# Output projection of layer 0 moved into the latent attention, one tile late; 112 candidates and an even split of marks in the channel mixer

## The reference

```
out = jnp.concatenate([out_a, out_b], axis=-1) @ w_out
...
x = layer_norm(ALPHA * x + out, ln1_g[0], ln1_b[0])

# peer, per head: the 16 best of each half, then the 16 best of their sums
t1, i1 = lax.top_k(s1, PEER_TOPK)
t2, i2 = lax.top_k(s2, PEER_TOPK)
cand = t1[..., :, None] + t2[..., None, :]          # 16 x 16
top, sel = lax.top_k(cand, PEER_TOPK)
gate = jax.nn.softmax(top)
y = sum over k of gelu(x . u_tab[idx_k]) * gate_k * v_tab[idx_k]
```

## Time and profile before

| what | value |
|---|---|
| median of the runs | 4629.32 us (4619.73 to 4639.67) |
| the profiled execution | 4627.48 us, span 4625.8 us, mean granted clock 0.909 |
| busy share of the span | PE 83%, PEld 61%, DVE 62%, ACT 21%, POOL 34% |
| DMA | 1189.86 MB, mean 257 GB/s |
| attention, 581.8 to 1011.8 us | 430 us, PE busy 322.6 us |
| gap to the channel mixer, 1012 to 1145 us | 133 us, PE busy 77.4 us |

### The profile page before, as it was taken

One profiled execution on the slowest core, in us unless ns is written; L12 is line 12 of the kernel. 1 busy time (PEld: TensorE's weight loads), 2 busy tenths in 40 slices (PEclk: granted clock), 3 DMA queues, 4 the chain that ended last, 5 costly groups with the idle time before them and its releaser, 6 DMA issues. The chain is left out here.

```text
span 4625.8 us, 50127 instructions
## 1 busy us (share of the span) xinstructions
PE 3833.2 (83%) x17006; PEld 2823.3 (61%) x17006; DVE 2862.4 (62%) x6195; ACT 952.8 (21%) x2541; POOL 1559.2 (34%) x1334
## 2 busy tenths in 40 slices
PE   9788867767988799979889488768889799889885
PEld 4577733333866677757667344456667677667664
DVE  0256522312898988857777422345998987667767
ACT  0133111111121244301011112211212444101101
POOL 0012024310054365545555000000352655455552
PEclk9899979888999899989999799969999899999997
DMA  3100157762487899989999364404787999899995
GB/s 122 40 19 13 44 149 209 187 189 80 164 314 269 314 409 417 415 335 396 392 401 390 137 236 146 160 19 147 253 295 290 385 417 416 343 388 403 392 400 193
DMA packets 368972, 1189.86 MB, mean 257 GB/s; under 512 B 33988, under 2 KB 152389, under 8 KB 340749
## 3 DMA queue, kind: packets, MB, share of 16 engines
q0 software_dynamic: 159840, 570.77, 32.7%
q1 hardware_dynamic: 194174, 538.35, 32.2%
q10 hardware_dynamic: 14704, 77.55, 4.1%
HBM read 1094.29 MB, written 87.73 MB: 256 GB/s over the span
## 5 line engine op out<-in xcount | busy, mean ns | idle before, releaser
L1878 POOL DMA_INDIRECT peer_ru<-in_u_rows,peer_expert x512 | 793.0, 1549 | 1200.8 <-DVE peer_dot L2153 903.5
L1993 PE MATMUL peer_bank<-region,peer_v 128*128 128x288 f32 x4096 | 1032.0, 416 | 154.0 <-DMA peer_v<-in_v 117.9
L1946 PE MATMUL peer_bank<-peer_xT,peer_u 128*128 128x288 f32 x4096 | 1041.4, 412 | 43.5 <-ACT peer_hidden L2059 43.5
L1993 PEld LDWEIGHTS peer_bank<-region,peer_v 128*128 128x128 f32 x4096 | 798.9, 196 | 387.0 <-DMA peer_v<-in_v 124.3
L1946 PEld LDWEIGHTS peer_bank<-peer_xT,peer_u 128*128 128x128 f32 x4096 | 779.5, 193 | 253.2 <-issue 46.9
L2143 DVE SCALAR_TENSOR_TENSOR y<-peer_rv,peer_weight,y 128x1024 f32<-128x1024 f32 x512 | 655.0, 1279 | 139.6 <-ACT peer_weight L2009 101.9
L1886 POOL DMA_INDIRECT peer_rv<-in_v_rows,peer_expert x512 | 552.9, 1080 | 268.1 <-issue 137.5
L2153 DVE CUSTOM_DVE_ANT_0 peer_ru<-peer_ru,x 128x1024 f32<-128x1024 f32 x512 | 622.4, 1216 | 24.1 <-DMA peer_ru<-in_u_rows,peer_expert 23.5
L2007 ACT ACTIVATE peer_act_g<-peer_dot 128x1 f32<-128x1 f32 x512 | 103.4, 202 | 1217.8 <-DVE peer_dot L2153 1209.0
L2273 DVE TENSOR_TENSOR region<-region,peer_bank 128x288 f32<-128x288 f32 x496 | 219.6, 450 | 168.2 <-PE peer_bank L1993 166.0
L1868 POOL MEMSET y<- 128x1024 f32 x4 | 3.7, 951 | 728.5 <-POOLq L143 728.5
(11 more groups left out here) (491 smaller groups left out, 4385.2 us busy)
## 6 DMA issues: line engine op xcount, KB each, us to landing
peer_u<-in_uT SPq DMA_DIRECT2D x128, 1024.0 KB, 8.9
peer_v<-in_v SPq DMA_DIRECT2D x64, 2048.0 KB, 13.8
mlstm_w_in<-in_w_in_o SPq DMA_DIRECT2D x30, 1792.0 KB, 7.3
mla_keys<-in_keysT SPq DMA_DIRECT2D x256, 144.0 KB, 4.4
scratch_early<-peer_hidden ACTq DMA_DIRECT2D x64, 576.0 KB, 9.1
scratch_grids<-region ACTq DMA_DIRECT2D x24, 1536.0 KB, 10.4
region<-scratch_grids SPq DMA_DIRECT2D x32, 1152.0 KB, 28.2
region<-scratch_early SPq DMA_DIRECT2D x64, 576.0 KB, 7.5
```

The lines of the kernel that those rows point to most:

```text
L1878: pool.indirect_dma_start(ru[:, n % U_ROWS, :], None, u_rows, bass.IndirectOffsetOnAxis(ap=expert[:, T, k:k + 1], axis=0)).then_inc(ru_in[ ...
L1946: mm = mmul(bank[:, 4 + i % 2, 0:TD], u[:, h % URING, i % 2, k, :], xT[:, k, :], start=k == 0, stop=k == KD - 1)
L1993: mm = mmul(bank[:, SUM_BANKS[m % 6], 0:TD], v[:, g % 2, j, c * P:(c + 1) * P], w[:, g % 2, j, :], start=j == 0, stop=j == GI - 1)
```

## The change

In the attention: `mla` becomes `mla_layer`, which loads its constants itself and does the output projection of a tile inside the next one but one in its order (tile 0's inside tile 1, and so on; those of tile 3 and SAMP follow the loop). `x` is allocated from the start (the linear mixer's scratch tiles are laid into it), so that the store and load of `x_mid` go. `w_out` comes in parts of 256 columns (1 MB) through two buffers: 20 loads, the first 14 issued by ACT, the rest by SP. The key ring has 4 slots, `oT` shares the memory of `wukT`, and the new rows of the samples are loaded in halves. The norms of the next tile move from the tile's start to places between heads 3 and 6 of the tile before. `ckv` and `kpe` are stored by SP.

In the channel mixer: 112 sums instead of 256 (for the first four of one list all 16 of the other, for the other twelve the first four), with more index work; and of the four row marks DVE makes two and ACT two.

```
-    RING, KRING = 6, 5
+    RING, KRING = 6, 4
+        def load_out(eng, n):
+            if n >= 2:
+                eng.wait_ge(o_prod, n - 1)
+            eng.dma_start(w_out[:, n % 2, :, :], w_out_dram[:, :, n % 4 * OC:(n % 4 + 1) * OC]).then_inc(wo_in[n % 2], 16)
...
+                def out_turn(t, at):
+                    pe.wait_ge(mix_in, 16 * (t + 1))
+                    pe.wait_ge(tile_ok, t + 1)
+                    for i in range(2):
+                        for k in range(4):
+                            mm = turn(bank[:, at[i], k * P:(k + 1) * P], mix[:, (4 * i + k) * P:(4 * i + k + 1) * P], C["ident"])
+                    mm.then_inc(o_turned, 1)
+                def out_part(t, c, at):
...
+                    pe.wait_ge(wo_in[n % 2], 16 * (n // 2 + 1))
+                    for k in range(KD):
+                        mm = mmul(bank[:, at, c % 2 * OC:(c % 2 + 1) * OC], mT[:, k, :], w_out[:, n % 2, k, :], start=k == 0, stop=k == KD - 1)
+                    mm.then_inc(o_prod, 1)
...
+                    past = pos - 2
+                    if past >= 0:
+                        out_turn(past, (4, 5))
...
+                    if past >= 0:
+                        out_part(past, 0, 1)
+                        out_part(past, 1, 1)
                     pe.wait_ge(roped, pos + 1)
...
+                    if past >= 0:
+                        out_part(past, 2, 3)
+                        out_part(past, 3, 3)
                     pe.wait_ge(qt_kept, 2 * (pos + 1))
...
+                out_turn(SAMP - 1, (4, 5))
+                for c in range(4):
+                    out_part(SAMP - 1, c, 1 + c // 2)
+                out_turn(SAMP, (6, 7))
+                for c in range(4):
+                    out_part(SAMP, c, 3 + c // 2)
... (ACT)
+                        if past >= 0:
+                            for n in (4 * past + 2, 4 * past + 3):
+                                load_out(act, n)
...
                     for i in range(H + 2):
+                        if i == 5:
+                            if past >= 0:
+                                norm_root(act, past)
+                            if t + 1 < SAMP:
+                                roots(pos + 1)
+                        if i == 7 and past >= 0:
+                            norm_shift(act, past)
+                        if i == 3 and past >= 0:
+                            for n in (4 * past + 4, 4 * past + 5):
+                                load_out(act, n)
... (DVE)
+                        add_out(past, (1, 3))
                     for h in range(H + 2):
+                        if h == 4:
+                            if past >= 0:
+                                norm_sums(past)
+                            if t + 1 < SAMP:
+                                squares(t + 1)
+                        if h == 6:
+                            if past >= 0:
+                                norm_scales(past)
+                            if t + 1 < SAMP:
+                                norms(pos + 1, t + 1)
+                        if h == 8 and past >= 0:
+                            norm_rows(past)
... (channel mixer)
+CANDS = 4 * PK + (PK - 4) * 4
-                    best16([(cand[r, h, :], cand2[r, h, :], top[r, h, :], sel[r, h, :]) for h in range(PH)])
+                    best16([(cand[r, h, 0:CANDS], cand2[r, h, 0:CANDS], top[r, h, :], sel[r, h, :]) for h in range(PH)])
-                    V.tensor_copy(abf[r], ab[r]).then_inc(diff, 1)
+                    ch(V.tensor_copy(abf[r], ab[r]))
+                    stt(abf[r, 0, :], abf[r, 1, :], -12.0, abf[r, 0, :], ALU.add, ALU.max)
+                    ch(stt(abf[r, 3, :], posf[r], 64.0, abf[r, 3, :], ALU.is_lt, ALU.mult))
+                    tt(abf[r, 1, :], abf[r, 2, :], abf[r, 3, :], ALU.add).then_inc(diff, 1)
...
-                    for i in range(3):
+                    for i in range(2):
                         tok = slice(4 * b + i, 4 * b + i + 1)
                         ins = V.tensor_scalar(rowhot[:, b % 4, i, :], C["iota"], picks[:, 0, tok], picks[:, 2, tok], ALU.is_equal, ALU.mult)
```

More of the change, by code:

```diff
@@ L179, with rwkv @@
 IN_TAIL = 4 * TILES
[L182 removed]
+def rwkv(nc, base, A, proj_b, mix, O, x):
     with Stage(nc, "rwkv") as st:
@@ L1145, in mla @@
         o_s = sb("o", [P, KV])
-        oT = sb("oT", [P, 2, H, NB * SEG])
+        mix, mT = sb("mix", [P, D]), sb("mT", [P, KD, P])
+        w_out = sb("w_out", [P, 2, KD, OC])
+        gain, shift = sb("gain", [P, D]), sb("shift", [P, D])
+        stats, mv = sb("stats", [P, 2, 6]), sb("mv", [P, 6])
         bank = st.banks("bank", 8)
@@ L1208, in _ @@
                     sp.dma_start(dst, src).then_inc(here, 16)
+                for dst, src in ((x[:, :, :], A["x0"].rearrange("(t p) d -> p t d", p=P)), (gain[:, :], A["ln1_g0"].partition_broadcast(P)),
+                                 (shift[:, :], A["ln1_b0"].partition_broadcast(P))):
+                    sp.dma_start(dst, src).then_inc(x_in, 16)
                 sp.dma_start(pages[:, :], A["page_table"]).then_inc(pin, 16)
@@ L1344, in _ @@
                                 pe.wait_ge(ex, n - 1)
+                            if i == 1 and past >= 0:
+                                pe.wait_ge(added, 2 * (past + 1))
                             mmul(bank[:, 2 + i % 2, 0:n_k], qT[:, i, :], KT[:, i, 0:n_k], start=True, stop=True).then_inc(sc, 1)
@@ L1529, in _, with keep_mixed, add_out, norm_sums @@
                     V.tensor_copy(kpad[:, 64:QH], kr[:, t, :]).then_inc(norm, 1)
+                def keep_mixed(t, at):
+                    dve.wait_ge(o_turned, t + 1)
+                    if t:
+                        dve.wait_ge(o_prod, 4 * t)
+                    V.tensor_copy(mT[:, 4:8, :].rearrange("p a b -> p (a b)"), bank[:, at, :]).then_inc(o_kept[1], 1)
+                def add_out(t, at):
+                    for i in range(2):
+                        dve.wait_ge(o_prod, 4 * t + 2 * i + 2)
+                        half = x[:, t, i * 512:(i + 1) * 512]
+                        st2(out=half, in0=half, scalar=ALPHA, in1=bank[:, at[i], :], op0=ALU.mult, op1=ALU.add).then_inc(added, 1)
+                    dve.wait_ge(added, 2 * (t + 1))
+                def norm_sums(t):
+                    V.bn_stats(stats[:, 0, :], x[:, t, 0:512])
+                    ch(V.bn_stats(stats[:, 1, :], x[:, t, 512:D]))
+                    ch(V.bn_aggr(mv[:, 0:2], stats[:, :, :]))
+                    tsc(mv[:, 2:3], mv[:, 1:2], 1e-5, None, ALU.add).then_inc(s_sum, 1)
+                def norm_scales(t):
+                    dve.wait_ge(s_root, t + 1)
+                    ch(V.reciprocal(mv[:, 4:5], mv[:, 3:4]))
+                    st2(out=mv[:, 5:6], in0=mv[:, 0:1], scalar=-1.0, in1=mv[:, 4:5], op0=ALU.mult, op1=ALU.mult).then_inc(s_sum, 1)
+                def norm_rows(t):
+                    dve.wait_ge(s_norm, t + 1)
+                    ch(tt(x[:, t, :], x[:, t, :], gain[:, :], ALU.mult))
+                    ch(tt(x[:, t, :], x[:, t, :], shift[:, :], ALU.add))
+                squares(SAMP)
+                norms(0, SAMP)
+                for pos, t in enumerate(ORDER):
+                    past = pos - 2
+                    cos, sin = angles(t)
                     dve.wait_ge(flipped, pos + 1)
@@ L2854, in _ @@
                 dve.wait_ge(x_ok, TILES)
-@contextmanager
-def consts(nc, name, A, C):
-    lo, hi = const_span(name)
-    with nc.sbuf_tensor(f"const_{name}", [P, hi - lo], F32) as tile:
-        load(nc, [(tile[:, :], A["consts"][:, lo:hi])])
-        yield C | const_views(tile, name)
 def build(nc, A, O):
```

265 lines of the change are left out of this document (132 added, 133 removed).

## The result

The changed kernel takes 4612.82 us (median of 17 runs, 4598.19 to 4623.01), the kernel before in the same series 4633.77: a ratio of 0.995, 95% interval 0.9939 to 0.9962. That is 21 us less, where 42 were forecast. The time lies 3 us above the forecast's own range (4562 to 4610) and inside the wider one that was to hold 8 cases in 10 (4545 to 4622); the size of the gain is half of what the sum said.

A forecast was written before the change was run, and what follows sets the result against it. No engine was taken as full; short waits from engine to engine bound the attention. Attention loop +60, the stretch after it −88 and mixer −14 made −42 us: 4587 us, own range 4562 to 4610, 8-in-10 range 4545 to 4622.

The forecast's parts named there:

- The gap: From PE's last attention matmuls (T0) to the channel mixer's first issue: 45 us against 133.4, so −88 us.
- the tail's 1.9, 7.2 and 27: After T0: tile 3's turn and copy 1.9 us, two projection parts at hand 7.2, six parts in three load rounds 27.
- the norms' waits: At the starts of tiles 1 to 3, PE's 7.14-us wait for DVE's norms shrinks to about 1: −18 us.
- the finals: In the channel mixer, each final over 112 candidates saves 5.3 us; two in PE's 13.2-us wait give −10.6 per layer.
- the dense finals: Three finals beside the gathered rows in the channel mixer: at most 10.5 us could go, taken as 0.
- the marks: In the mixer's dense part, DVE loses 0.35 us a block and ACT gains 0.88: +3.4 us per layer.
- The clock's +3: In the attention loop, less idle time might speed PE, but longer DVE stalls add idle: +3 us, bounds −6 and +9.
- DMA in the loaded stretch: Two of a tile's four parts load where DMA share is 0.93, with four key slots: +12 us, bounds 0 and 40.
- The step on the moved norms: In the attention, norm work on DVE ahead of the maxima of heads 4 and 6 delays PE: +24 us, bounds 0 and 24.
- Rival (B): Attention tiles become a DMA loop: late keys and values cost 47 us, the shorter ring 18; 4640 us, chance 0.09.
- (A): Rival: in the attention, the DVE, DMA and clock delays (+24, +12, +3) are absorbed; 4548 us, chance 0.16.
- (C): Rival: the mixer gives nothing, ACT's marks come last on 18 blocks, +11 us for two layers; 4612 us, chance 0.15.

## Why the prediction was wrong

The mechanism of the sum held, term by term but for two. The gap closed by 85.4 (forecast 88; the tail's 1.9, 7.2 and 27 add up to 36.1, not to the 36.5 of the sum, and PE ended 39.9 us behind T0); the products in tiles 1 to 3 run as 7.07 and 7.2 to 7.5 us a pair, with 0.8 to 1.2 us of wait for the third part (0.8); the norms' waits went, at −18 as summed, and those behind the maxima came, at 18.9 rather than 24; the mixer gave 18.4 (14), with the finals at 6.9 and 6.3 rather than 10.6 a layer, the dense finals at 2 rather than 0, and the marks at about 0 rather than +3.4. The clock's +3 can't be told apart: the granted clock of the loop fell from 0.92 to 0.89, and what that cost is part of the prices below.

The step that failed is *DMA in the loaded stretch*: +12, with bounds 0 and 40. By single removal the parts' traffic is worth 28.6 us of loop and the fifth slot 18.3, together 47, above even the upper bound. Two things were mis-sized. I let the DVE stalls make room for the parts ("about as much time"), and so took half of 24; and I priced the lost slot by a load's 4 us in each tile and then left it nearly out. The run with four slots in the kernel before shows that it costs 20 us with no parts at all: the lead was one unit, and the shorter ring took all of it.

The step on the moved norms was right in its kind and too large in its worth: taking the delay away gave 10.6 to 12.6 us in three pairs of kernels (454.6 to 444.0, 431.2 to 418.6, 412.5 to 401.9), since the key steps took back 15 to 18 us each time. DVE's 24 and DMA's 12 made 36 in the sum; the three single removals make 57.5 (28.6, 18.3 and 10.6). The 21.5 between them is the loop's excess over the forecast, 20 us. With the 395.5 us of work the three make 453.0, and 454.6 was measured. The fit is in part luck: the 28.6 holds the 3.1 us of waits for parts, of which the sum already had 2.4 among the products. And the forecast was as near as it was because its two errors have opposite signs: the DMA step was 35 us too low, the norms' step 13 too high.

Rival (B) named the mechanism, late keys and the shorter ring, and priced it at 65 us (47 and 18); by removal it cost 47 (28.6 and 18.3). Its sign, waits of several microseconds for keys inside a tile, was there (2.78 and 3.97), but not its 54 us: PE's waits for keys grew by 16.3, and the rest of the price stood in stretched products. Its counter-argument (half of the parts' bytes find room in the first third of a tile) was sound: the run with the other half moved there, too, gave 23.4 of the 28.6 back. The Trainium skill ("DMA: Bandwidth & Descriptors", Issuing engines are not separate DMA queues) says that another issuer gives no other DMA; this case shows it at its hardest, since ACT's 2 MB, issued between SP's page loads, made a 5.43-us key step 19.5 us long. (A) is out: by it the loop would have grown by 22 us, and it grew by 81. The median is (C)'s 4612, by chance: PE's waits in the dense part still name DVE's marks, and the mixer gained 18.4 us where (C) had it lose 11.

What stays open: the tail, where PE waits 4.6 us for parts (1.96, 1.60 and 1.02) that SP issues one behind the other, was not tried with its loads earlier or larger. Nor was a ring of more than five slots.

## What to carry to other kernels

A transfer that is put into a loop is priced by the stretch in which it is issued: look for the window with the low DMA share and issue it there, which was worth 23 us here for the same bytes. A ring should hold one consumer step and at least one unit of the next: that one slot was worth 17 to 20 us here, and a slot taken to make room is a cost of its own, to be measured alone. And where an engine is delayed in front of a resource that is nearly full, the waits that the profile shows for that engine can overstate what removing them will give, here by about two to one.

## What the runs showed of the hardware

A late load can cost more than its wait. In tile 1 of the changed kernel six key records between two waits, of 2.78 and 3.97 us, took 2.76 us at a granted clock of 1.00; the six behind the second took 5.33 at 0.50, the lower of the two levels. It is no rule: a key step stretched to 7.62 us was followed by values at 0.60 (7.43 us for 32 records), one stretched to 8.36 us by values at 1.00 (4.57).

Key loads of 144 KB that SP issued right behind 2 MB from ACT landed after 6.6 to 12.7 us; with the 2 MB issued 14 us earlier they landed after 2.2 to 5.1. And a late load needn't show as a wait: in the kernel with four slots 17.6 us of the loop's 20 stood as busy time of PE.
